# Two of the four weight sums of each FFN block by accumulating DMAs instead of VectorE adds

## The chip, the cores and the metric

The kernel runs on one core of one Trainium2 chip. The metric is the device time of one execution in microseconds, from three executions. A profile of one execution shows every instruction of the core's engines: PE is TensorE's matmuls and PEld its weight loads, DVE is VectorE, ACT is ScalarE, POOL is GpSimd, and SP is SyncE, which here only issues DMAs.

## What is computed

Two encoder layers over 256 tokens of width 2048: a recurrent and dilated-attention mixer, then a differential-attention mixer, each followed by a dense SwiGLU FFN with 5632 hidden columns. The change touches the FFN alone:

```python
D_MODEL = 2048
SEQ = 256
D_FF = -(-8 * D_MODEL // (3 * 256)) * 256

def swiglu(h, w_gate, w_up, w_down):
    return (jax.nn.silu(h @ w_gate) * (h @ w_up)) @ w_down
```

## The kernel before, in words

Everything is float32. A weight tile is 512 x 512 (1 MiB, 128 partitions of 2048 elements). Each tile is loaded from HBM by SP into a buffer `raw`, split by ACT into a rounded high part `w_hi` (four buffers, `hi`) and by DVE into the remainder `w_lo` (three buffers, `lo`), and TensorE makes three passes: high times high, high times low, low times high. A pass over 128 tokens is 4 matmuls of 128x512.

The FFN has 11 blocks of 512 hidden columns per layer. The first gate and up block of a layer is made ahead of the loop; a *body* (`block(body)` on each engine, 10 per layer, 20 in all) multiplies block j by its down weights (units `d0` to `d3`) and makes gate and up of block j+1. The contraction over 2048 is four row groups of 512, named by a digit: `g0` to `g3` are the gate tiles, `u0` to `u3` the up tiles. Groups 2 and 3 are plain *dense units* (both token halves t = 0 and 1, 24 matmuls). Groups 0 and 1 go by a seven-product scheme on the 2x2 blocks (token half by row group; row group by gate or up): products `P1` to `P7` of 12 matmuls each. `P1`, `P2`, `P3` use the plain tiles g0, g1, u1. The other four use sums and differences of the four tiles, made by `form` on DVE, each one add or subtract of 128x2048: P5 and P6 in g0's buffer, P7 (from u0 and u1) in u0's buffer, P4 (the sum of all four, with g1 as the last) in g0's buffer again.

The matching sums of the activations are made once per layer (`left_sums` on GpSimd). The partial products are combined per body: `copy_first` and `copy_fifth` on ACT, `second`, `third` and `corner` on DVE, `spreads` on GpSimd.

The order of the work in a body is written out by hand: the table `ENTRIES` sets TensorE's order and numbers the units, the calls `high(...)` and `low(...)` set ACT's and DVE's, and `LOADS` sets the order of SP's loads. All engines work their queues strictly in order. Five tile buffers (`raw0` to `raw2`, `gx`, `queries`) are handed out by `place_loads`: each load takes the buffer whose last reader comes first, and waits for that reader (`released`). The accumulator banks are `acc00`, `acc01`, `acc10`, `acc11` (second digit: token half) and `sc`, `pv`. P7 goes into `acc01`. `third` reads it there, and only then may the token half 1 of the up column write that bank; `open_bank` holds this wait:

```python
if name == first_of(column, t):
    n = body.gate if column == "g" else body.up
    pe.wait_ge(acc_free[n % 2][t], n // 2)
    if t:
        pe.wait_ge(sum_done, body.sum["S2" if column == "g" else "S3"])
```

Lines of the profile that matter: L931 is ACT's `hi`, L1527 DVE's `lo`, L1540, L1542, L1545 and L1547 are the DVE adds that form the tiles of P5, P6, P7 and P4, L1826 is `second`, L1832 `third`, L1840 `corner`, L1263 a matmul of a dense unit, L1276 one of the products P1 to P7, L796 SP's load, L2030 and L2032 GpSimd's `spreads`.

Of the kernel before, what the change touches and what calls it, by code (L numbers as in the profile page):

```python
# [94 lines left out]
        self.b = self.block_e = self.block_m = None  # L95

ENTRIES = ("P1", "P5", "P3", "P6", "g2", "P2", "P7", "P4", "u3", "g3", "u2", "d0", "d1", "d2", "d3")
LOADS = ("u1", "u0", "g0", "g2", "g1", "u3", "g3", "u2", "d0", "d1", "d3", "d2")
EARLY = ("g0", "u0")  # L100
FORMS = ("P5", "P6", "P7", "P4")
SUMS = ("S2", "S3")
PLAIN = {"P1": "g0", "P2": "g1", "P3": "u1"}

# [176 lines left out]
def hi(u):  # L281
    return Task("hi", u=u)
# [244 lines left out]
def place_loads(plan):  # L527

    count, free = [0] * BLOCK_RAW, [()] * BLOCK_RAW

    def take(key, buffers, released):
        buf = min(buffers, key=lambda i: max((when for _, _, when in free[i]), default=-1))
        count[buf] += 1
        plan.place[key] = Place(buf, count[buf], [wait[:2] for wait in free[buf]])
        free[buf] = released

    def released(body, name):
        lo_of = {entry: ("lo", u + 1, u) for entry, u in body.u.items()}
        form_of = {entry: ("form", n, body.u[entry] - 1) for entry, n in body.form.items()}
        return {"g0": (lo_of["P4"],), "u0": (lo_of["P7"],), "u1": (lo_of["P3"], form_of["P7"]),  # L540
                "g1": (lo_of["P2"], form_of["P4"])}.get(name) or (lo_of[name],)

    for part in plan.parts:
        for task in part.tasks or ():
            if task.kind == "early_load":
                take((task.src.index, task.what), range(RAW, BLOCK_RAW), released(task.src, task.what))
            elif task.kind == "tile_unit" or task.kind == "half" and task.t == 0 and task.passes[0] == 0:
                take(task.slot.u, range(RAW), (("lo", task.slot.u + 1, task.slot.u),))
        for body in part.bodies or ():
            for name in loads_of(body):  # L550
                take((body.index, name), range(BLOCK_RAW), released(body, name))
            for name in FORMS:
                plan.formed[body.u[name]] = body.form[name]
            for name in ENTRIES:
                weight = {"P4": "g0", "P5": "g0", "P6": "g0", "P7": "u0"}.get(name) or PLAIN.get(name, name)
                plan.place[body.u[name]] = plan.place[body.index, weight]

def trunk(nc, x, norm_mix_pre, norm_mix_post, norm_ffn_pre, norm_ffn_post,
# [9 lines left out]
    with ExitStack() as ctx:  # L569
# [144 lines left out]
        rg_sum = sem("rg_sum")  # L714
        rg_hi = sem("rg_hi")
        form_done = sem("form_done")
        left_part = sem("left_part")
        left_sum = sem("left_sum")
        left_hi_done = sem("left_hi_done")
# [65 lines left out]
        def _(sp):  # L785
# [5 lines left out]
            def load(key, src):  # L791

                place = plan.place[key]
                for what, value in place.free:
                    sp.wait_ge(lo_done if what == "lo" else form_done, value)
                sp.dma_start(raw[place.buf][:, :, :], src.rearrange("(k p) n -> p k n", p=P)).then_inc(landed[place.buf], 16)  # L796

            def input_chunk(c):
# [102 lines left out]
        def _(act):  # L901
# [18 lines left out]
                for kt in range(c * KT, (c + 1) * KT):  # L920
                    tile_hi(kt)

            def hi(u, formed=0):
                place = plan.place[u]
                if formed:
                    act.wait_ge(form_done, formed)
                else:
                    act.wait_ge(landed[place.buf], 16 * place.count)
                if u >= HI:
                    act.wait_ge(unit_done, u - HI + 1)  # L930
                act.activation(w_hi[u % HI][:, :, :], raw[place.buf][:, :, :], ACT.Copy).then_inc(hi_done, 1)  # L931
# [217 lines left out]
            def block(body):  # L1149

                def high(name):
                    hi(body.u[name], body.form.get(name, 0))

                def high_next(name):
                    u = body.base + len(ENTRIES) + ENTRIES.index(name)
# [30 lines left out]
                block_hi(body)  # L1186
                high("P2")
                high("P7")
                high("P4")
                high("u3")  # L1190
                high("g3")
                high("u2")
                high("d0")
# [304 lines left out]
        def _(dve):  # L1498
# [31 lines left out]
            def form(body, name):  # L1530

                def weight(which):
                    place = plan.place[body.index, which]
                    dve.wait_ge(landed[place.buf], 16 * place.count)
                    return raw[place.buf][:, :, :]

                g0 = raw[plan.place[body.index, "g0"].buf][:, :, :]
                if name == "P5":
                    up = weight("u0")
                    dve.tensor_tensor(g0, up, g0, ALU.subtract).then_inc(form_done, 1)  # L1540
                elif name == "P6":
                    dve.tensor_tensor(g0, weight("u1"), g0, ALU.subtract).then_inc(form_done, 1)  # L1542
                elif name == "P7":
                    up = weight("u0")
                    dve.tensor_tensor(up, weight("u1"), up, ALU.subtract).then_inc(form_done, 1)  # L1545
                else:
                    dve.tensor_tensor(g0, weight("g1"), g0, ALU.subtract).then_inc(form_done, 1)  # L1547

            def operand_lo(e, m, hi_ap, lo_ap):
                dve.wait_ge(t_hi, m + 1)  # L1550
# [257 lines left out]
            def block(body):  # L1808
# [11 lines left out]
                def second():  # L1820

                    dve.wait_ge(unit_done, body.u["P6"] + 1)
                    dve.wait_ge(copied[0], body.index + 1)
                    if not body.first:
                        dve.wait_ge(spread, 2 * body.index)
                    dve.tensor_tensor(spare[1], acc[1][1][:, :], spare[0], ALU.add).then_inc(sum_done, 1)  # L1826

                def third():

# [4 lines left out]
                def corner(column, t, other, out):  # L1834
# [2 lines left out]
                    wait_last(dve, body, column, t)  # L1837
                    if (column, t) != ("g", 0):
                        dve.wait_ge(spread, 2 * body.index + (1 if (column, t) == ("u", 0) else 2))
                    dve.tensor_tensor(out, acc[n % 2][t][:, :], other, ALU.add).then_inc(acc_free[n % 2][t], 1)  # L1840

                def gated(t):

# [11 lines left out]
                low("P3")  # L1855
                low("P6")
                low("g2")
                form(body, "P7")
                second()
                low("P2")  # L1860
                form(body, "P4")
                low("P7")
                low("P4")
                low("u3")
                third()
                low("g3")
                low("u2")
# [30 lines left out]
        def _(pool):  # L1898
# [100 lines left out]
            def left_sums(b, layer):  # L1999
# [12 lines left out]
                whole(spare[1], 0, 1)  # L2012
                whole(spare[0], 1, 1)
                pool.wait_ge(left_part, done + 2)
                pool.tensor_tensor(spare[0], spare[0], spare[1], ALU.add).then_inc(left_sum, 1)
                whole(spare[2], 0, 0)
                pool.wait_ge(left_part, done + 3)
                pool.tensor_tensor(spare[3], spare[2], spare[1], ALU.subtract).then_inc(left_sum, 1)
                pool.wait_ge(left_sum, done + 2)
                pool.tensor_tensor(spare[2], spare[0], spare[2], ALU.subtract).then_inc(left_sum, 1)  # L2020
                whole(spare[1], 1, 0)
                pool.wait_ge(left_part, done + 4)
                pool.wait_ge(left_sum, done + 3)
                pool.tensor_tensor(spare[1], spare[1], spare[2], ALU.subtract).then_inc(left_sum, 1)

            def spreads(body):

# [6 lines left out]
            for section in plan.parts:  # L2034
                for task in section.tasks or ():
                    task_of(task)
                for body in section.bodies or ():
                    spreads(body)

# [39 lines left out]
```

## Time and profile before

| | |
|---|---|
| timed executions | 2217.74, 2217.95, 2219.11 us (median 2217.95) |
| span of the profiled execution, first to last instruction | 2217.0 us (the profile gives no other time of its own for it) |
| TensorE busy, granted clock | 99% of the span, 0.998 of full speed |
| DVE, ACT, GpSimd busy | 76%, 53%, 14% |
| one body in the steady state | 63.65 us (P1 at 743.80 to P1 at 807.46) |
| loads | 395 MiB, SP's queue, 54.8% of the 16 DMA engines |

The span stands for the time: it lies 0.95 us under the median. A matmul record overlaps the next one, so TensorE's busy share does not show how dense it is; the distance from start to start does. Idle time of an engine that nothing waits for costs nothing.

### The profile page before, as it was taken

The page shows a single profiled execution, that of the slowest core. Times are in us where ns is not written, and L with a number is a line of the kernel's source. Part 1 is how long each engine was busy: PE and PEld are TensorE (multiplying, and loading weights), DVE is VectorE, ACT ScalarE, POOL GpSimd, SP SyncE. Part 2 cuts the span into 40 slices and gives each one's busy share as a digit, 9 for nine tenths or more (in the row PEclk, how much of TensorE's full clock was granted, in tenths as well). Part 3 has the DMA queues.
Part 4 walks back from the last instruction along what each step waited for, and adds up shares of the span by engine and source line. Part 5 has one row for each costly group of instructions (what it writes and reads, how often), then busy time and mean ns, then how long its engine had stood idle before and what let it go on. Part 6 is the DMA issues. An engine that isn't in the chain of part 4 may idle for free.

```text
span 2217.0 us, 26301 instructions
## 1 busy us (share of the span) xinstructions
PE 2199.2 (99%) x10011; PEld 1810.1 (82%) x10011; DVE 1692.9 (76%) x1686; ACT 1173.1 (53%) x1330; POOL 304.2 (14%) x247
## 2 busy tenths in 40 slices
PE   8999999999999999999999999999999999999998
PEld 7888888888888888888887787788888888888886
DVE  5587467988888888888755655778888898888886
ACT  6677544654454454444655555546555454544543
POOL 0851000300000000000021001004000000000001
PEclk9999999999999999999999999999999999999999
DMA  9555446456656555564564445455656545566552
GB/s 309 186 169 169 166 133 209 152 191 228 227 190 208 191 172 186 192 228 175 167 209 152 152 152 166 169 190 179 228 190 218 198 169 175 189 228 227 190 190 95
DMA packets 213883, 416.52 MB, mean 188 GB/s; under 512 B 12328, under 2 KB 14976, under 8 KB 213248
## 3 DMA queue, kind: packets, MB, share of 16 engines
q1 hardware_dynamic: 213040, 414.29, 54.8%
q8 instruction: 81, 1.33, 0.2%
q10 hardware_dynamic: 720, 0.56, 0.1%
q14 instruction: 42, 0.34, 0.0%
HBM read 412.73 MB, written 2.10 MB: 187 GB/s over the span
## 4 chain that ended last, share of the span: by engine, by line
PE 97%; DVE 1%; DMA 1%; issue 0%; ACT 0%; SPq 0%; POOLq 0%; POOL 0%; DVEq 0%; ACTq 0%
PE acc L1263 73%; PE acc L1276 12%; PE tp L1292 2%; PE sc L1276 2%; PE pv L1276 2%; PE sc L1374 1%; DMA raw<-in_ev_w_in 1%; PE pv L1403 1%; PE sc L1370 1%; PE pv L1398 1%; PE sc L1353 0%; PE pv L1353 0%; DVE w_lo L1527 0%; SPq L789 0%; PE pv L1292 0%
## 5 line engine op out<-in xcount | busy, mean ns | idle before, releaser
L1527 DVE TENSOR_TENSOR w_lo<-raw,w_hi 128x2048 fp32r<-128x2048 f32 x301 | 689.5, 2304 | 57.7 <-PE acc L1263 40.8
L931 ACT ACTIVATE w_hi<-raw 128x2048 fp32r<-128x2048 f32 x301 | 572.9, 1911 | 152.4 <-PE acc L1263 105.9
L1263 PE MATMUL acc<-w_hi,h_hi 128*128 128x512 f32 x1576 | 432.6, 396 | 3.8 <-ACT h_hi L903 3.8
L1263 PE MATMUL acc<-w_lo,h_hi 128*128 128x512 f32 x1576 | 423.1, 390 | 0.0
L1263 PE MATMUL acc<-w_hi,h_lo 128*128 128x512 f32 x1576 | 422.1, 390 | 0.0
L1263 PEld LDWEIGHTS acc<-w_lo,h_hi 128*128 128x128 f32 x1576 | 296.0, 188 | 62.7
L1263 PEld LDWEIGHTS acc<-w_hi,h_lo 128*128 128x128 f32 x1576 | 295.6, 188 | 61.9
L1263 PEld LDWEIGHTS acc<-w_hi,h_hi 128*128 128x128 f32 x1576 | 291.2, 188 | 63.4 <-issue 6.9
L931 ACT ACTIVATE w_hi<-gx 128x2048 fp32r<-128x2048 f32 x70 | 134.4, 1920 | 221.0 <-DVE gx L1540 83.8
L931 ACT ACTIVATE w_hi<-queries 128x2048 fp32r<-128x2048 f32 x70 | 134.4, 1920 | 220.4 <-DVE queries L1540 83.9
L1263 PE MATMUL acc<-w_hi,y_hi 128*128 128x512 f32 x832 | 224.6, 392 | 0.7 <-ACT y_hi L1135 0.7
L1263 PE MATMUL acc<-w_lo,y_hi 128*128 128x512 f32 x832 | 222.7, 389 | 0.0
L1263 PE MATMUL acc<-w_hi,y_lo 128*128 128x512 f32 x832 | 222.5, 389 | 0.0
L2030 POOL TENSOR_TENSOR probT<-probT,rgx 128x512 f32<-128x512 f32 x20 | 40.8, 2039 | 1137.1 <-ACT rgx L1170 1137.1
L1607 DVE TENSOR_TENSOR yacc<-acc,yacc 128x512 f32<-128x512 f32 x208 | 138.9, 686 | 75.8 <-PE acc L1263 75.8
L1263 PEld LDWEIGHTS acc<-w_lo,y_hi 128*128 128x128 f32 x832 | 156.1, 188 | 32.7
L1263 PEld LDWEIGHTS acc<-w_hi,y_lo 128*128 128x128 f32 x832 | 156.2, 188 | 32.6
L1263 PEld LDWEIGHTS acc<-w_hi,y_hi 128*128 128x128 f32 x832 | 155.0, 188 | 33.2 <-issue 1.9
L1527 DVE TENSOR_TENSOR w_lo<-gx,w_hi 128x2048 fp32r<-128x2048 f32 x70 | 160.0, 2286 | 7.9 <-ACT w_hi L931 7.9
L1527 DVE TENSOR_TENSOR w_lo<-queries,w_hi 128x2048 fp32r<-128x2048 f32 x70 | 160.0, 2286 | 7.9 <-ACT w_hi L931 7.9
L1840 DVE TENSOR_TENSOR prob<-acc,prob 128x512 f32<-128x512 f32 x20 | 13.8, 692 | 100.3 <-PE acc L1263 100.3
L1276 PE MATMUL acc<-w_hi,lefts 128*128 128x512 f32 x320 | 88.1, 397 | 0.0
(240 smaller groups left out, 2321.8 us busy)
## 6 DMA issues: line engine op xcount, KB each, us to landing
raw<-in_ffn_w_gate SPq DMA_DIRECT2D x68, 1024.0 KB, 5.8
raw<-in_ffn_w_up SPq DMA_DIRECT2D x68, 1024.0 KB, 5.2
raw<-in_ffn_w_down SPq DMA_DIRECT2D x48, 1024.0 KB, 7.7
raw<-in_od_w_in SPq DMA_DIRECT2D x48, 1024.0 KB, 5.1
raw<-in_ev_w_in SPq DMA_DIRECT2D x37, 1024.0 KB, 5.4
queries<-in_ffn_w_down SPq DMA_DIRECT2D x20, 1024.0 KB, 6.9
gx<-in_ffn_w_down SPq DMA_DIRECT2D x20, 1024.0 KB, 7.0
raw<-in_ev_w_out SPq DMA_DIRECT2D x16, 1024.0 KB, 5.1
```

The source lines that it names most:

```text
L931: act.activation(w_hi[u % HI][:, :, :], raw[place.buf][:, :, :], ACT.Copy).then_inc(hi_done, 1)
L1263: mm = pe.matmul(acc[n % 2][t][:, :], operand(lhs, a, k, t), w[:, k, :], start=first and k == 0 and j == 0, stop=last and k == KT - 1 and ...
L1276: mm = pe.matmul(bank, a[:, k, :], w[:, k, :], start=start and k == 0 and j == 0, stop=stop and k == KT - 1 and j == 2)
L1292: ins = pe.transpose(dst, src, ident[:, :])
L1370: mm = pe.matmul(sc[:, t, :], q[:, kt, t * P:(t + 1) * P], k[:, kt, task.i % 2, :], start=True, stop=True)
L1374: mm = pe.matmul(sc[:, :, :].rearrange("p m t -> p (m t)"), q[:, kt, t * P:(t + 1) * P], k[:, kt, :, :].rearrange("p m t -> p (m t)"), sta ...
L1398: mm = pe.matmul(pv[:, 0, t * HD:(t + 1) * HD], probT[:, j, t * P:(t + 1) * P], v[:, j, task.i * HD:(task.i + 1) * HD], start=j == 0, stop ...
L1403: mm = pe.matmul(pv[:, 0, 0:CV], flat_pt[:, j * P:(j + 1) * P], v[:, j, hd * CV:(hd + 1) * CV], start=j == 0, stop=j == 1)
L1527: dve.tensor_tensor(w_lo[u % LO][:, :, :], raw[plan.place[u].buf][:, :, :], w_hi[u % HI][:, :, :].bitcast(F32), ALU.subtract).then_inc(lo_ ...
L1607: dve.tensor_tensor(y, a, y, ALU.add).then_inc(acc_free[n % 2][t], 1)
L1840: dve.tensor_tensor(out, acc[n % 2][t][:, :], other, ALU.add).then_inc(acc_free[n % 2][t], 1)
L2030: pool.tensor_tensor(spare[1], spare[1], spare[3], ALU.add).then_inc(spread, 1)
```

## The change

The signs of u0 and g1 (and of the activations and outputs that go with them) are turned, so that all four weight tiles are sums: P5 is u0 + g0, P6 adds u1, P7 is u0 + u1, P4 is P6's tile + g1. P7's and P4's tiles are no longer formed by DVE. GpSimd issues one DMA for each, from one buffer to another in SBUF, that adds its source to its destination: `up_sum` (u1 onto u0, after P5's tile is formed) and `whole_sum` (g1 onto g0's buffer, after the low part of P6's tile has been taken). ACT's `hi` of P7 and P4 waits for the DMA's semaphore, and so do the loads that reuse u1's and g1's buffers. In the orders of TensorE, ACT and DVE, P4 and u3 change places, so that P4 comes one dense unit later. Signs in `left_sums`, `second` and `corner` follow.

```diff
-ENTRIES = ("P1", "P5", "P3", "P6", "g2", "P2", "P7", "P4", "u3", "g3", "u2", "d0", "d1", "d2", "d3")
+ENTRIES = ("P1", "P5", "P3", "P6", "g2", "P2", "P7", "u3", "P4", "g3", "u2", "d0", "d1", "d2", "d3")
-FORMS = ("P5", "P6", "P7", "P4")
+FORMS = ("P5", "P6")
+TRANSFERS = ("P7", "P4")
...
+        form_of.update({entry: (entry, 16 * (body.index + 1), body.u[entry] - 1) for entry in TRANSFERS})
...
-                sp.wait_ge(lo_done if what == "lo" else form_done, value)
+                sp.wait_ge(transferred[what] if what in TRANSFERS else lo_done if what == "lo" else form_done, value)
...
-            def hi(u, formed=0):
+            def hi(u, formed=0, moved=None):
                 place = plan.place[u]
-                if formed:
+                if moved:
+                    act.wait_ge(*moved)
+                elif formed:
...
                if name == "P5":
                     up = weight("u0")
-                    dve.tensor_tensor(g0, up, g0, ALU.subtract).then_inc(form_done, 1)
-                elif name == "P6":
-                    dve.tensor_tensor(g0, weight("u1"), g0, ALU.subtract).then_inc(form_done, 1)
-                elif name == "P7":
-                    up = weight("u0")
-                    dve.tensor_tensor(up, weight("u1"), up, ALU.subtract).then_inc(form_done, 1)
+                    dve.tensor_tensor(g0, up, g0, ALU.add).then_inc(form_done, 1)
                 else:
-                    dve.tensor_tensor(g0, weight("g1"), g0, ALU.subtract).then_inc(form_done, 1)
+                    dve.tensor_tensor(g0, weight("u1"), g0, ALU.add).then_inc(form_done, 1)
...
                 low("g2")
-                form(body, "P7")
                 second()
                 low("P2")
-                form(body, "P4")
                 low("P7")
+                low("u3")
                 low("P4")
-                low("u3")
                 third()
...
+            def up_sum(body):
+
+                place = plan.place[body.index, "u1"]
+                pool.wait_ge(landed[place.buf], 16 * place.count)
+                place = plan.place[body.index, "u0"]
+                pool.wait_ge(landed[place.buf], 16 * place.count)
+                pool.wait_ge(form_done, body.form["P5"])
+                pool.dma_start(raw[place.buf][:, :, :], raw[plan.place[body.index, "u1"].buf][:, :, :], accum_op=ALU.add).then_inc(transferred["P7"], 16)
+
+            def whole_sum(body):
+
+                place = plan.place[body.index, "g1"]
+                pool.wait_ge(landed[place.buf], 16 * place.count)
+                pool.wait_ge(lo_done, body.u["P6"] + 1)
+                pool.dma_start(raw[plan.place[body.index, "g0"].buf][:, :, :], raw[place.buf][:, :, :], accum_op=ALU.add).then_inc(transferred["P4"], 16)
...
                 for body in section.bodies or ():
+                    up_sum(body)
+                    whole_sum(body)
                     spreads(body)
```

TensorE's order in the second body, from P7 to the start of g3, before. `acc01` is the bank that `third` reads, and `sum_done` is the semaphore that `third` raises.

```order
L1276 MATMUL acc01<-w_hi2,lefts 128x512 [waits hi_done,left_lo_done,acc_free01]
...
L1276 MATMUL acc11<-w_hi3,h_hi 128x512 [waits hi_done]
...
L1276 MATMUL acc11<-w_lo2,h_hi 128x512 [waits lo_done]
...
L1263 MATMUL acc00<-w_hi0,h_hi 128x512 [waits hi_done]
...
L1263 MATMUL acc01<-w_hi0,h_hi 128x512 [waits hi_done,acc_free01,sum_done]
```

And in the change:

```order
L1282 MATMUL acc01<-w_hi2,lefts 128x512 [waits hi_done,left_lo_done,acc_free01]
...
L1269 MATMUL acc00<-w_hi3,h_hi 128x512 [waits hi_done]
...
L1269 MATMUL acc01<-w_hi3,h_hi 128x512 [waits hi_done,acc_free01,sum_done]
...
L1282 MATMUL acc11<-w_hi0,h_hi 128x512 [waits hi_done]
...
L1282 MATMUL acc11<-w_lo0,h_hi 128x512 [waits lo_done]
```

The unit that writes acc01 again (u3) now follows P7 directly; before, the 12 matmuls of P4 (acc11) lay between.

DVE's order at the same place, from the tile of P6 to `third`, before:

```order
L1542 TENSOR_TENSOR gx<-raw0,gx 128x2048 [waits landed0]
L1527 TENSOR_TENSOR w_lo0<-raw0,w_hi1 128x2048 [waits unit_done,hi_done]
L1527 TENSOR_TENSOR w_lo1<-gx,w_hi2 128x2048 [waits unit_done,hi_done]
L1527 TENSOR_TENSOR w_lo2<-raw1,w_hi3 128x2048 [waits unit_done,hi_done]
L1545 TENSOR_TENSOR queries<-raw0,queries 128x2048 [waits landed0,landed4]
L1826 TENSOR_TENSOR probT<-acc11,prob 128x512 [waits spread,copied0,unit_done]
L1527 TENSOR_TENSOR w_lo0<-raw2,w_hi0 128x2048 [waits unit_done,hi_done]
L1547 TENSOR_TENSOR gx<-raw2,gx 128x2048 [waits landed2]
L1527 TENSOR_TENSOR w_lo1<-queries,w_hi1 128x2048 [waits unit_done,hi_done]
L1527 TENSOR_TENSOR w_lo2<-gx,w_hi2 128x2048 [waits unit_done,hi_done]
L1527 TENSOR_TENSOR w_lo0<-raw1,w_hi3 128x2048 [waits unit_done,hi_done]
L1832 TENSOR_TENSOR rgx<-acc01,probT 128x512 [waits sum_done,unit_done]
```

And in the change:

```order
L1548 TENSOR_TENSOR raw2<-queries,raw2 128x2048 [waits landed4]
L1533 TENSOR_TENSOR w_lo0<-queries,w_hi1 128x2048 [waits unit_done,hi_done]
L1533 TENSOR_TENSOR w_lo1<-raw2,w_hi2 128x2048 [waits unit_done,hi_done]
L1533 TENSOR_TENSOR w_lo2<-raw1,w_hi3 128x2048 [waits unit_done,hi_done]
L1827 TENSOR_TENSOR probT<-prob,acc11 128x512 [waits spread,copied0,unit_done]
L1533 TENSOR_TENSOR w_lo0<-gx,w_hi0 128x2048 [waits unit_done,hi_done]
L1533 TENSOR_TENSOR w_lo1<-raw0,w_hi1 128x2048 [waits unit_done,hi_done]
L1533 TENSOR_TENSOR w_lo2<-raw1,w_hi2 128x2048 [waits unit_done,hi_done]
L1533 TENSOR_TENSOR w_lo0<-raw2,w_hi3 128x2048 [waits unit_done,hi_done]
L1833 TENSOR_TENSOR rgx<-acc01,probT 128x512 [waits sum_done,unit_done]
```

The two adds are gone, and the last `lo` ahead of `third` is now P4's (from raw2, the buffer that the DMA adds into), where before it was u3's.

GpSimd's order in the change, two bodies, where before only the two TENSOR_TENSOR rows stood:

```order
L2032 DMA raw0<-queries 128x2048 [waits form_done,landed0,landed4]
L2039 DMA raw2<-gx 128x2048 [waits lo_done,landed3]
L2045 TENSOR_TENSOR probT<-probT,rgx 128x512 [waits sum_done,copied1]
L2047 TENSOR_TENSOR rgx<-rgx 128x512 [waits spread]
L2032 DMA raw1<-raw0 128x2048 [waits form_done,landed1,landed0]
L2039 DMA gx<-raw2 128x2048 [waits lo_done,landed2]
```

Nothing on GpSimd waits for a DMA's end. On SP, the load of g3 waits for the DMA of P7, and one of the loads of d0, d1 for that of P4, where before g3 and u2 waited for DVE's adds.

## Rows read from the trace of the kernel before

**Rows 1.** The page, busy time of each engine over the span.

```profile
PE 2199.2 (99%) x10011; PEld 1810.1 (82%) x10011; DVE 1692.9 (76%) x1686; ACT 1173.1 (53%) x1330; POOL 304.2 (14%) x247
```

**Rows 2.** Waits of TensorE, the whole span: us in total, times, longest us.

```profile
PE acc L1263 <- ACT h_hi L903: 3.8, 1, 3.8
...
PE acc L1276 <- DVE w_lo L1527: 1.4, 2, 0.7
PE acc L1263 <- ACT y_hi L1135: 0.7, 2, 0.3
```

**Rows 3.** Windows: us, then PE, PEld, DVE, ACT, POOL busy, PEclk, DMA share, GB/s.

```profile
743.80:807.46 63.66, 63.66 (x288) 52.65 (x286) 53.38 (x38) 31.27 (x21) 5.35 (x2) 1.00 0.57 198
807.46:871.11 63.65, 63.65 (x288) 52.64 (x285) 53.38 (x38) 31.27 (x21) 5.35 (x2) 1.00 0.57 198
...
752.70:766.00 13.30, 13.30 (x60) 10.96 (x59) 13.13 (x8) 7.87 (x5) 0.00 (x0) 1.00 0.82 278
```

**Rows 4.** Timeline of TensorE in one body: start us, us, instruction.

```profile
743.80 1.17 PE L1276 MATMUL sc<-w_hi,h_hi 128*128 128x512 f32 x4
...
763.04 1.10 PE L1276 MATMUL acc<-w_hi,lefts 128*128 128x512 f32 x4
...
765.85 1.08 PE L1276 MATMUL acc<-w_hi,h_hi 128*128 128x512 f32 x4
...
768.58 1.07 PE L1263 MATMUL acc<-w_hi,h_hi 128*128 128x512 f32 x4
769.49 1.07 PE L1263 MATMUL acc<-w_lo,h_hi 128*128 128x512 f32 x4
```

**Rows 5.** Timeline of DVE, same body.

```profile
735.29 2.28 DVE L1540 TENSOR_TENSOR gx<-queries,gx 128x2048 f32<-128x2048 f32 x1
...
748.22 2.29 DVE L1527 TENSOR_TENSOR w_lo<-gx,w_hi 128x2048 fp32r<-128x2048 f32 x1
750.42 2.28 DVE L1527 TENSOR_TENSOR w_lo<-raw,w_hi 128x2048 fp32r<-128x2048 f32 x1
752.62 2.28 DVE L1545 TENSOR_TENSOR queries<-raw,queries 128x2048 f32<-128x2048 f32 x1
...
757.89 2.28 DVE L1547 TENSOR_TENSOR gx<-raw,gx 128x2048 f32<-128x2048 f32 x1
...
766.70 0.68 DVE L1832 TENSOR_TENSOR rgx<-acc,probT 128x512 f32<-128x512 f32 x1
```

**Rows 6.** Timeline of ACT, same body: high parts of P7 and of P4.

```profile
754.94 1.93 ACT L931 ACTIVATE w_hi<-queries 128x2048 fp32r<-128x2048 f32 x1 [1.83 <-DVE queries L1545]
760.21 1.93 ACT L931 ACTIVATE w_hi<-gx 128x2048 fp32r<-128x2048 f32 x1 [3.34 <-DVE gx L1547]
```

**Rows 7.** Timeline of SP's queue, same body: loads of u3 and g3.

```profile
752.73 0.37 SPq L796 DMA_DIRECT2D raw<-in_ffn_w_up  x1
754.98 0.37 SPq L796 DMA_DIRECT2D raw<-in_ffn_w_gate  x1
```

**Rows 8.** The page: the load queue, and the loads' time to landing.

```profile
q1 hardware_dynamic: 213040, 414.29, 54.8%
...
raw<-in_ffn_w_up SPq DMA_DIRECT2D x68, 1024.0 KB, 5.2
```

**Rows 9.** Timeline of GpSimd, same body.

```profile
778.95 2.04 POOL L2030 TENSOR_TENSOR probT<-probT,rgx 128x512 f32<-128x512 f32 x1 [58.22 <-ACT rgx L1170]
781.07 3.31 POOL L2032 TENSOR_TENSOR rgx<-rgx 128x512 f32<-128x512 f32 x1
```

**Rows 10.** Timeline of the first body of layer 0.

```profile
431.66 2.28 DVE L1527 TENSOR_TENSOR w_lo<-gx,w_hi 128x2048 fp32r<-128x2048 f32 x1
431.80 1.20 PE L1276 MATMUL acc<-w_lo,lefts 128*128 128x512 f32 x4 [0.71 <-DVE w_lo L1527]
...
436.17 0.37 SPq L796 DMA_DIRECT2D raw<-in_ffn_w_up  x1
...
444.71 1.10 PE L1276 MATMUL acc<-w_hi,lefts 128*128 128x512 f32 x4
```

More of the change, by code:

```diff
@@ L716, in trunk @@
         form_done = sem("form_done")
+        transferred = {name: sem(f"transferred_{name}") for name in TRANSFERS}
         left_part = sem("left_part")
@@ L1151, in high @@
                 def high(name):
-                    hi(body.u[name], body.form.get(name, 0))
+                    moved = (transferred[name], 16 * (body.index + 1)) if name in TRANSFERS else None
+                    hi(body.u[name], body.form.get(name, 0), moved)
                 def high_next(name):
@@ L1188, in block @@
                 high("P7")
+                high("u3")
                 high("P4")
-                high("u3")
                 high("g3")
@@ L1825, in second @@
                         dve.wait_ge(spread, 2 * body.index)
-                    dve.tensor_tensor(spare[1], acc[1][1][:, :], spare[0], ALU.add).then_inc(sum_done, 1)
+                    dve.tensor_tensor(spare[1], spare[0], acc[1][1][:, :], ALU.subtract).then_inc(sum_done, 1)
                 def third():
@@ L1839, in corner @@
                         dve.wait_ge(spread, 2 * body.index + (1 if (column, t) == ("u", 0) else 2))
-                    dve.tensor_tensor(out, acc[n % 2][t][:, :], other, ALU.add).then_inc(acc_free[n % 2][t], 1)
+                    dve.tensor_tensor(out, acc[n % 2][t][:, :], other, ALU.add if column == "g" else ALU.subtract).then_inc(acc_free[n % 2][t], 1)
                 def gated(t):
@@ L2014, in left_sums @@
                 pool.wait_ge(left_part, done + 2)
-                pool.tensor_tensor(spare[0], spare[0], spare[1], ALU.add).then_inc(left_sum, 1)
+                pool.tensor_tensor(spare[0], spare[0], spare[1], ALU.subtract).then_inc(left_sum, 1)
                 whole(spare[2], 0, 0)
@@ L2019, in left_sums @@
                 pool.wait_ge(left_sum, done + 2)
-                pool.tensor_tensor(spare[2], spare[0], spare[2], ALU.subtract).then_inc(left_sum, 1)
+                pool.tensor_tensor(spare[2], spare[0], spare[2], ALU.add).then_inc(left_sum, 1)
                 whole(spare[1], 1, 0)
```

## The prediction

> **What bounds the kernel now.** I read the page first: TensorE is busy 99% of the span, DVE 76%, GpSimd 14% [rows 1]. Busy time does not say how dense TensorE is, so I took TensorE's waits next. Over the whole span it waits for another engine some 6 us in all, and for DVE 1.4 us, in two places [rows 2]. Those two are the first body of each layer, where P3's low pass waits for its `lo` [rows 10], ahead of everything that the change takes off DVE. The windows then give the steady body: 63.65 us, the same twice, TensorE busy throughout, at the full granted clock (2.4 GHz) [rows 3]. A pass of 4 matmuls takes 0.91 us from start to start, a token half of a dense unit three passes, 2.72 us, and P4 2.73 us [rows 4]. Nothing in a body waits for DVE, though DVE is busy 53.4 of 63.7 us. So TensorE's own rate sets the time, and the change leaves its matmuls as they are. What can move the time is only a wait that the change makes.
>
> **Removed: two adds per body on DVE.** 2 x 2.28 us [rows 5], 91 us over 20 bodies. They lie beside matmuls, and TensorE's waits show nobody who gets them back: worth nothing. DVE now stands idle ahead of `second`, which needs P6's product.
>
> **Added: the transfer for P7.** It may start when P5's tile is formed, at 735.29 + 2.28 = 737.6 [rows 5]. ACT takes P7's tile at 754.94 [rows 6], so 17 us cover it. Without that cover its whole time would fall on P7. The load of g3 waits for it too, and now goes out right behind u3's load (752.73) instead of at 754.98 [rows 7]. That matters below.
>
> **Added and moved: the transfer for P4.** Here cover is short, because of what queues behind the wait. ACT waits for the transfer; DVE's `lo` of P4 waits for ACT; `third` stands behind that `lo` on DVE; and `third` must have read acc01 before u3's second token half may write it. u3 now starts where P4 did, at 765.85, and its second half 2.72 us later, at 768.57. Counted back from there: `third` 0.68 and hand-over 0.06; `lo` 2.20 to the next start; hi 1.93 and hand-overs 0.07 [rows 5, 6]. The transfer must have landed by 763.6. It is issued when `lo` of P6 ends, 748.22 + 2.29 = 750.5, so by 750.6. **It has 13.0 us.** By the same chain `lo` of u3 precedes that of P4 on DVE, another 2.20 us, so u3's tile must have landed by 761.4. Its load is issued at 752.73: **it has 8.7 us**, and takes 5.2 today [rows 8].
>
> **What a transfer costs.** The trace of before has no accumulating DMA and no DMA out of SBUF. The nearest row is the 1 MiB load. The queue's 54.8% of the span for 414.29 MB is 3.07 us of the 16 engines for one load, and 5.2 - 3.07 = 2.1 us is fixed [rows 8]. Low end: the price of a load, 5.2 us. An accumulate reads two tiles and writes one, so I take twice the engine time, 6.14 us, and the 2.1 us, with 0.4 us for GpSimd's issue as SP's rows have it [rows 7]: 8.6 us with the engines to itself. High end: GpSimd's own add, 3.31 us for a quarter of a tile, 13.3 us for a whole one [rows 9]. I take the middle value, since the load is the nearer row.
>
> The Trainium skill (DMA: Bandwidth & Descriptors, "Anatomy of one DMA") gives a GpSimd-issued DMA 2.0 us plus bytes by 436 GB/s. Two reads would come to 6.8 us by an estimate from it, and the transfer would then be hidden; its 4.4 us for a plain MiB is less than the 5.2 of the row.
>
> The engines are not idle there: from 752.7 to 766.0 the DMA share is already 0.82 [rows 3]. Two bounds for the sharing, since no row shows two busy queues. With **equal shares**, the transfer has 1.7 us alone before u3's load comes, and its other 4.4 us run at half speed: 0.4 + 2.1 + 1.7 + 8.9 = 13.1 us against 13.0, late by 0.1; u3's load takes 2.1 + 6.14 = 8.3 of its 8.7. With the **transfer ahead**, it is in time, and u3's load finds the engines taken for 0.4 + 6.14 - 2.1 = 4.4 us: 9.6 against 8.7, late by 0.9. I take the middle, 0.5 us per body: 18 steady bodies, 9.0 us.
>
> **The first bodies.** There `lo` of P6 ends at 431.66 + 2.28 = 433.9 and P7 starts at 444.71 [rows 10], 10.8 us later, where the steady body has 12.5 (750.5 to 763.04 [rows 4, 5]). Cover is 1.8 us shorter for both, with hand-overs: 1.9 late with equal shares, 2.7 with the transfer ahead. Middle 2.3, twice: 4.6 us.
>
> **At nothing, and why.** ACT's wait holds g3's high part behind it, which TensorE needs after u3 and P4, 8.2 us later. SP's load that waits for P4's transfer is one of d0 and d1, used over 15 us on. GpSimd issues and goes on; its `spreads` end at 784.4 [rows 9], ahead of the next P5 tile. Sums instead of differences cost DVE the same row. The load queue's other tiles come up to 6 us later and have that much.
>
> **The sum.** 2217.0 + 9.0 + 4.6 = 2230.6 us of span. The span lay 0.95 us under the median of the runs, so I forecast **2231.5 us**, 0.6% slower. About 0.2% (4.4 us) is what a measurement of this kernel can tell from no change.
>
> **Rivals.**
>
> *Not slower: the transfer is hidden* (0.36). If the engine time of an accumulate is 5 us or less, equal shares land it by 0.4 + 2.1 + 5 + 3.3 = 10.8 us, over 2 us early, and the first bodies are at most about 0.5 to 2 us late. For it: the read of SBUF may be quicker than that of HBM, and my own case misses the deadline by tenths. Against it: two reads, and a busy DMA window. Time 2217 to 2221. It decides at some 5.5 us of engine time.
>
> *Much slower: the DMA's adder is slow* (0.16). From 9.2 us of engine time (three loads) the transfer takes 0.4 + 2.1 + 1.7 + 2 x 7.5, 19.2 us with equal shares, 6 us late; with the transfer ahead 11.7 us, in time, but u3's load is 4 us late. 20 bodies: +80 to +125, so 2298 to 2343, and above 2370 at GpSimd's own rate. Only the far row [rows 9] speaks for it.
>
> *Late descriptors* (0.08). GpSimd's two adds of equal size take 2.04 and 3.31 us [rows 9], so something holds it at times, and DVE is busy 13.13 of 13.30 us in the window [rows 3]. If GpSimd must wait one DVE instruction (2.28 us) before it can start the DMA, all 20 bodies are 2.3 us later than my sum: +46, 2277. Against it: DVE has a pause of over 2 us ahead of `second` now.
>
> The Trainium skill (SBUF — State Buffer, "Who interferes with whom") has GpSimd blocked by DVE for such instructions only where GpSimd reads SBUF, and takes descriptor writing to be spared by adds with two SBUF inputs; so by the page this rival would not come about, and no row here shows a descriptor being written.
>
> *Faster* (0.02). Freed DVE time could at most give back TensorE's waits for it, 1.4 us [rows 2]: 2216.5, inside the noise. More than 4.4 us would need an effect that no row shows.
>
> **How the numbers follow.** The forecast's case, late by a few tenths to some two us per body (2222 to 2260), has 0.38. Slower by over 0.2% is 0.38 + 0.16 + 0.08, less 0.02 for the edge at 2222: 0.60. Within 0.2%: 0.36 and that 0.02: 0.38. Faster: 0.02. The range runs from the hidden case, 2216.5, to 2290, which takes in the late descriptors and leaves out nearly all of the slow adder and the 0.02 below. Slower cases hold the most; the likeliest one's own range is 2222 to 2260.
>
> **What would show it.** TensorE's waits should have a new row, a dense matmul waiting for `third` on DVE, about 18 of equal length near 0.5 us and two longer, and the body should read some 64.1 us. ACT's wait ahead of P4's high part should end on the DMA, and that DMA should take 12 to 14 us from issue to landing, the one for P7 8 to 9. A body of 63.65 us with P4's transfer under 13 us shows the hidden case. Both transfers over 13 us show the slow adder, P7's being nearly alone. A wait ahead of u3's high part on its load, with the transfer in time, shows the transfer-ahead sharing. I am wrong in the chain itself if TensorE waits elsewhere, such as on g3 or the down tiles. A body under 63.5 us would mean that something sets the rate that I take as fixed.

## The result, and the profile after

The change takes **2241.76 us** (median of 4 runs, 2241.51 to 2242.12), the kernel before 2217.93 beside it: 1.0107 times as long, 95% interval 1.0095 to 1.0119. The profiled execution took 2242.12 us, with a span of 2240.3, 23.3 us above that of before.

The page of the change, its busy times, queues and issues:

```profile
PE 2207.8 (99%) x10011; PEld 1808.7 (81%) x10011; DVE 1607.8 (72%) x1646; ACT 1168.8 (52%) x1330; POOL 339.0 (15%) x287
...
q1 hardware_dynamic: 213040, 414.29, 53.6%
q0 software_dynamic: 5760, 41.95, 10.1%
...
raw<-in_ffn_w_up SPq DMA_DIRECT2D x80, 1024.0 KB, 7.6
...
raw<-raw POOLq DMA_DIRECT2D x16, 1024.0 KB, 7.0
...
queries<-gx POOLq DMA_DIRECT2D x8, 1024.0 KB, 8.2
```

DVE lost 85 us of work against [rows 1], the 40 adds that the diff takes away. Queue q0 is new: 40 transfers, whose 10.1% of the span makes 5.66 us of the 16 engines for one, in the mean of P7's and P4's. P7's land in 7.0 us (the raw<-raw row), P4's in 8.2. The loads of `ffn_w_up`, u3's among them, went in the median from 5.2 us to landing [rows 8] to 7.6; u3's alone take 9.1 to 10.8.

TensorE's waits in the change, against [rows 2]:

```profile
PE acc L1269 <- issue: 9.5, 19, 0.7
PE acc L1269 <- DVE w_lo L1533: 5.9, 7, 1.1
PE acc L1269 <- ACT h_hi L906: 2.4, 1, 2.4
...
PE acc L1282 <- DVE w_lo L1533: 1.4, 2, 0.7
PE acc L1269 <- ACT w_hi L936: 1.0, 1, 1.0
```

Nineteen short waits for "issue" (time in which the profile names nothing that TensorE waited for), seven for a low part, and one for a high part are new. The 1.4 us of P3's low pass stay. Windows from one P7 to the next, in the change (columns as in [rows 3]); the first row is the first body of layer 0, the last that of layer 1:

```profile
443.49:511.43 67.94, 65.85 (x285) 53.62 (x284) 49.14 (x35) 32.13 (x22) 7.09 (x4) 0.97 0.71 228
511.43:575.71 64.28, 63.91 (x286) 52.57 (x284) 49.14 (x35) 31.03 (x22) 7.08 (x4) 1.00 0.73 229
639.99:705.93 65.94, 64.23 (x286) 52.48 (x284) 49.14 (x35) 32.10 (x22) 7.09 (x4) 1.00 0.72 225
...
1579.62:1645.73 66.11, 64.25 (x286) 52.41 (x285) 49.14 (x35) 31.02 (x21) 7.11 (x4) 1.00 0.74 233
```

Read so for all 20 bodies, against the same stretches of before (63.65 us, the first bodies 63.72): 13 steady bodies are longer by 0.54 to 0.80 us (0.66 in the mean), 5 by 1.2 to 2.3 (9.4 us together), the first bodies by 4.2 and 2.4. That is 8.6 + 9.4 + 6.6 = 24.6 us, and all that lies ahead of the first P7 came out 1.2 us shorter (443.49 against 444.71). So the 23.3 us are all in the FFN bodies. This is how one of the 13 loses its time, from the timeline of layer 1's third body, sorted by engine:

```profile
1699.54 0.85 POOL L2039 DMA_DIRECT2D gx<-raw  x1 [12.23 <-DVE w_lo L1533]
...
1701.03 0.37 SPq L799 DMA_DIRECT2D queries<-in_ffn_w_up  x1
1701.49 1.29 SPq L799 DMA_DIRECT2D raw<-in_ffn_w_gate  x1
...
1710.33 1.92 ACT L936 ACTIVATE w_hi<-queries 128x2048 fp32r<-128x2048 f32 x1 [7.12 <-DMA queries<-in_ffn_w_up]
1712.15 1.90 ACT L936 ACTIVATE w_hi<-gx 128x2048 fp32r<-128x2048 f32 x1
...
1712.28 2.29 DVE L1533 TENSOR_TENSOR w_lo<-queries,w_hi 128x2048 fp32r<-128x2048 f32 x1 [3.82 <-ACT w_hi L936]
1714.49 2.28 DVE L1533 TENSOR_TENSOR w_lo<-gx,w_hi 128x2048 fp32r<-128x2048 f32 x1
1716.69 0.68 DVE L1833 TENSOR_TENSOR rgx<-acc,probT 128x512 f32<-128x512 f32 x1
...
1715.96 1.07 PE L1269 MATMUL acc<-w_hi,h_lo 128*128 128x512 f32 x4
1717.48 1.17 PE L1269 MATMUL acc<-w_hi,h_hi 128*128 128x512 f32 x4 [0.45 <-issue]
```

GpSimd issues P4's transfer at 1699.54; it lands at 1707.8 (8.2 us). u3's load is issued at 1701.03 and lands 9.3 us later, at 1710.3, and ACT has waited 7.12 us for it, not for the transfer. From there it is the chain of the prediction: u3's high part, its low part, P4's low part, `third`, and TensorE starts u3's second token half 1717.48, when `third` (which ends at 1717.37) has read acc01.

Why the load took 9.3 us is in the windows of the same body:

```profile
1699.54:1700.90 1.36, 1.36 (x7) 1.09 (x6) 1.36 (x1) 1.36 (x2) 0.85 (x1) 1.00 0.00 0
1701.00:1706.50 5.50, 5.50 (x26) 4.56 (x25) 3.13 (x3) 2.21 (x2) 0.00 (x0) 1.00 1.07 185
1707.50:1710.00 2.50, 2.50 (x13) 2.07 (x12) 0.96 (x1) 0.00 (x0) 0.00 (x0) 1.00 1.04 402
```

### The profile page after: what moved, and what is told of

It is laid out like the page before. It is cut to its first block, busy times and chain, and to the rows that moved or that the text cites. A ratio compares the mean times of both kernels' runs of the same rounds, so it can differ in the third digit from the quotient of the medians.

```text
span 2240.3 us, 26321 instructions
## 1 busy us (share of the span) xinstructions
PE 2207.8 (99%) x10011; PEld 1808.7 (81%) x10011; DVE 1607.8 (72%) x1646; ACT 1168.8 (52%) x1330; POOL 339.0 (15%) x287
## 3 DMA queue, kind: packets, MB, share of 16 engines
q0 software_dynamic: 5760, 41.95, 10.1%
## 4 chain that ended last, share of the span: by engine, by line
PE 90%; DMA 4%; DVE 3%; ACT 1%; issue 1%; SPq 1%; ACTq 0%; POOLq 0%; POOL 0%; DVEq 0%
PE acc L1269 71%; PE acc L1282 9%; DMA raw<-in_ffn_w_up 3%; PE tp L1298 2%; PE sc L1282 2%; DVE w_lo L1533 2%; PE pv L1282 2%; PE sc L1380 1%; ACT w_hi L936 1%; PE pv L1409 1%; PE sc L1376 1%; PE pv L1404 1%; DMA raw<-in_ev_w_in 1%; DVE gx L1548 0%; PE sc L1359 0%
## 5 line engine op out<-in xcount | busy, mean ns | idle before, releaser
L1533 DVE TENSOR_TENSOR w_lo<-raw,w_hi 128x2048 fp32r<-128x2048 f32 x303 | 696.9, 2304 | 155.3 <-ACT w_hi L936 96.7
L1533 DVE TENSOR_TENSOR w_lo<-queries,w_hi 128x2048 fp32r<-128x2048 f32 x68 | 155.4, 2285 | 16.5 <-ACT w_hi L936 13.9
L1043 ACT ACTIVATE probT<-tp 128x256 f32<-128x256 f32 (+1 forms) x48 | 21.9, 456 | 110.5 <-PE pv L1409 64.3
```

What stands on the lines that cost most here:

```text
L1043: act.activation(flat_pt[:, 0:cols], flat_tp[:, 0:cols], ACT.Copy).then_inc(tp_free[task.e % 2], 1)
L1533: dve.tensor_tensor(w_lo[u % LO][:, :, :], raw[plan.place[u].buf][:, :, :], w_hi[u % HI][:, :, :].bitcast(F32), ALU.subtract).then_inc(lo_ ...
```

## The experiments

Theory A: P4's transfer holds the DMA engines, u3's load waits behind it, and the chain over `third` passes that on. B: not the transfer, but g3's load crowds u3's, since P7's transfer releases it 0.5 us behind u3's instead of 2.2. C: the order, with `third` behind P4's low part, costs by itself. Ratios are to the kernel before, run on the same chip.

### Parts of the change alone

```diff
-FORMS = ("P5", "P6")
-TRANSFERS = ("P7", "P4")
+FORMS = ("P5", "P6", "P7", "P4")
+TRANSFERS = ()
...
                 low("g2")
+                form(body, "P7")
                 second()
                 low("P2")
+                form(body, "P4")
                 low("P7")
...
-                    up_sum(body)
-                    whole_sum(body)
```

Both sums by DVE. 

> Undoes both transfers: DVE forms P7 and P4 again, at the places they had before, as sums; the turned signs and P4 behind u3 stay. A (P4's transfer takes the engines from u3's load): 2217.9, within 0.1% of before, u3's load back at 5.2 us. B (g3's load, released earlier by P7's transfer, crowds u3's load): 2217.9 too, since g3's load waits for DVE again. C (the order costs: third behind the low part of P4, a unit later): some 0.6 us per body stay, 2229 or more.

Measured 1.0006 (0.9997 to 1.0015), `ffn_w_up` loads 5.2 us. With P4's half of this edit alone (P7 by transfer):

> Only P7's sum by transfer; P4's by DVE as before, but P4 behind u3. A: no transfer near u3's load, so it lands in under 8.7 us and the time is 2218 to 2220. B: g3's load still goes out 0.5 us behind u3's, so u3's load stays slow (over 8.7 us) and most of the 24 us stay, 2235 or more.

Measured 0.9998 (0.9989 to 1.0007). With P7's half alone (P4 by transfer):

> Only P4's sum by transfer; P7's by DVE as before, which sends g3's load out some 2 us later than in the change. A: u3's load still finds the engines taken until 7.3 us behind the issue of the transfer, every body is late as in the change, 2235 to 2242. B: u3's load lands in time, 2218 to 2222. In between, near 2230, if the transfer makes the common 0.6 us per body and g3's load the bodies with 2.3 us.

Measured 1.0104 (1.0089 to 1.0120). The queue of the transfers in the run with P7's alone, then in the one with P4's alone:

```profile
q0 software_dynamic: 2880, 20.97, 4.7%
```

```profile
q0 software_dynamic: 2880, 20.97, 5.5%
```

Over spans of 2215.5 and 2241.4 us, that is 5.2 us of the 16 engines for one of P7's transfers and 6.2 us for one of P4's, the same kind of sum on the same number of bytes, but with u3's load issued just behind it.

The three settle it between A, B and C. C is out by the first. P7's transfer is free, and P4's alone costs all. B falls with the second, in whose timeline g3's load still goes out 0.46 us behind u3's, and u3's tile is there 5.3 us after its issue:

```profile
1683.03 0.37 SPq L799 DMA_DIRECT2D queries<-in_ffn_w_up  x1
1683.49 0.45 SPq L799 DMA_DIRECT2D raw<-in_ffn_w_gate  x1
...
1688.36 1.92 ACT L936 ACTIVATE w_hi<-queries 128x2048 fp32r<-128x2048 f32 x1 [3.15 <-DMA queries<-in_ffn_w_up]
```

### The chain over third

```diff
                 low("u3")
+                third()
                 low("P4")
-                third()
```

> The change with two of DVE's instructions swapped: third ahead of the low part of P4. A: u3's load and its low part are as late as in the change, but third no longer waits for them through P4's low part; the bodies with 0.6 us lose it, those whose low part of u3 comes too late for TensorE keep 0.6 to 1.3 us: 2224 to 2229. If the stall is elsewhere than in third: unchanged, 2241 to 2242.

Measured 1.0037 (1.0023 to 1.0052), 2227.15 us, within the expectation. TensorE's waits of this run have no "issue" row any more:

```profile
PE acc L1269 <- DVE w_lo L1533: 5.2, 6, 1.1
...
PE acc L1269 <- ACT w_hi L936: 0.9, 1, 0.9
```

So the 9.5 us that the change's profile puts down to "issue" were waits for `third`. What is left is u3's low part, late in the first bodies and in those where u3's load takes over 10 us (10.3 to 10.7 in this run).

### Holding the load, holding the transfer

g3's load held until u3's has landed:

```diff
                 for what, value in place.free:
                     sp.wait_ge(...)
+                if isinstance(key, tuple) and key[1] == "g3":
+                    early = plan.place[key[0], "u3"]
+                    sp.wait_ge(landed[early.buf], 16 * early.count)
                 sp.dma_start(raw[place.buf][:, :, :], ...)
```

> The change with one more wait on SP: g3's load goes out once u3's load has landed. A: u3's load still starts behind the transfer, but then has the engines alone and lands some 0.4 us sooner in the common bodies (10.8 to 10.4 us behind the transfer's issue) and 1.9 us sooner in those where it took over 10 us (12.3 to 10.4): 2222 to 2228, and no body with 2.3 us. If the 10 us loads have another cause than g3's load: 2234 or more. B alone (transfer harmless): u3's load under 6 us, 2218.

Measured 1.0094 (1.0079 to 1.0109), 2239.40 us: a miss for the 2222 to 2228 of A, and inside its alternative. The common bodies gained 0.1 to 0.2 us, and the long ones stayed, so the 10 us loads are not g3's doing either. Windows of one of them in this run, where u3's load is the only DMA left:

```profile
636.00:637.50 1.50, 1.50 (x8) 1.24 (x7) 0.56 (x1) 0.00 (x0) 0.00 (x0) 1.00 1.09 415
637.50:638.00 0.50, 0.50 (x4) 0.42 (x3) 0.00 (x0) 0.00 (x0) 0.00 (x0) 1.00 0.42 156
638.25:639.25 1.00, 1.00 (x6) 0.80 (x6) 0.00 (x0) 0.00 (x0) 0.00 (x0) 1.00 0.07 12
```

Nearly all of the load is done by 638; the rest has a share of 0.07, about 1/16, so I read it as one engine that ran late and brings the last pieces alone. Loads of over 10 us come in the same five bodies (the first, fourth and seventh of layer 0, the second and fifth of layer 1) in the change, in this run and in the swap above. In the change alone, the ninth body of layer 1 has a fairly long load too, of 9.8 us. Their cause stays open.

P4's transfer held until u3's load has landed:

```diff
                 pool.wait_ge(lo_done, body.u["P6"] + 1)
+                late = plan.place[body.index, "u3"]
+                pool.wait_ge(landed[late.buf], 16 * late.count)
                 pool.dma_start(...)
```

> The change with P4's transfer held until u3's load has landed. A: u3's load is back at 5 to 8 us and in time, but the transfer lands 8.2 us behind it, 15.5 to 18.5 us behind the low part of P6 where 13.0 is the budget: 2.5 to 5.5 us late in each of 20 bodies, 2268 to 2330, TensorE waiting for third, and ACT for the transfer. If the chain over third does not bind: under 2230.

Measured 1.0509 (1.0493 to 1.0524), 2331.83 us, 1.8 us beyond the far end of the expectation. Now ACT waits for the transfer and TensorE behind it (rows of one body; the wait is again `third`):

```profile
1763.37 1.92 ACT L936 ACTIVATE w_hi<-queries 128x2048 fp32r<-128x2048 f32 x1 [3.06 <-DMA queries<-in_ffn_w_up]
1772.29 1.92 ACT L936 ACTIVATE w_hi<-gx 128x2048 fp32r<-128x2048 f32 x1 [7.00 <-DMA gx<-raw]
...
1777.23 2.05 PE L1269 MATMUL acc<-w_hi,h_hi 128*128 128x512 f32 x4 [3.09 <-issue]
```

The wait itself is 3.1 us; the four matmuls behind it take 2.05 us instead of 1.08, with the granted clock at its lower level (1.2 GHz). The twenty waits sum to 71.9 us of the 113 lost. The mean granted clock of the run is 0.979, of the one of before 0.998, and 0.019 of 2331 us is 44 us: about the rest, by this estimate.

The same hold, with `third` ahead of P4's low part:

> P4's transfer held until u3's load has landed, and third ahead of P4's low part on DVE. Then only TensorE's own start of P4, 2.7 us behind that of u3's second half, waits for the transfer, and third is off the chain: budget about 18.7 us against 15.5 to 18.5. A: 2218 to 2222, the whole cost gone with both transfers kept. If the transfer's place costs something else (the down tiles' loads behind it): 2225 or more.

Measured 1.0052 (1.0035 to 1.0068), 2230.33 us: outside the 2218 to 2222, though not for the reason that its alternative gives. All 18 steady bodies are free of waits (63.65 us each); the rest is in the first bodies, where P7 starts sooner behind P6's low part and the held transfer comes too late for P4 itself:

```profile
PE acc L1282 <- ACT w_hi L936: 6.3, 2, 3.8
```

So I held it in the steady bodies alone (the two lines under `if not body.first:`):

> Both transfers kept, third ahead of P4's low part, and P4's transfer held until u3's load has landed, but in the 18 steady bodies alone; in the first body of each layer it starts when it can. A: the steady bodies have no wait, as with the hold in all bodies, and the first bodies are late as with third first alone, 2.3 and 1.3 us, without the 2.7 to 4.0 us and the half clock behind them that the hold made there: 2219 to 2223. It can't beat the kernel before, whose steady bodies are TensorE's own 63.65 us. If the hold moves the down tiles' loads so that first bodies suffer from it too: 2226 or more.

Measured 1.0022 (1.0013 to 1.0031), 2223.11 us, 0.1 us above the expectation. A steady body of it, to be read against [rows 3]:

```profile
511.42:575.07 63.65, 63.65 (x285) 52.64 (x284) 49.24 (x35) 31.16 (x21) 7.08 (x4) 1.00 0.73 231
```

That is before's rate again with both transfers in place. It does not beat the kernel before: in the steady bodies TensorE has no gap left to close, and the first bodies keep their waits.

### What the transfer costs, and how the engines share

P4's transfer as a plain copy (g1 over the tile), which leaves out one add per element and so changes P4's product:

```diff
-  pool.dma_start(<g0's buffer>, <g1's buffer>, accum_op=ALU.add)
+  pool.dma_start(<g0's buffer>, <g1's buffer>)
```

> P4's transfer copies g1 over the tile instead of adding it, with the same bytes written; P4's product is then that with g1 alone, and one add per element is left out. If the adding sets the 6.1 us of the engines: a copy takes about what a load does, 3.0 us, u3's load lands some 6 to 7 us behind its issue, inside its budget, and the time is 2218 to 2221. If the rows of 8 KB through GpSimd's queue are slow by themselves: the same 6.1 us, and 2241.

Measured 0.9999 (0.9989 to 1.0008), with u3's load landing in about 6.2 us, inside its 8.7. From its page:

```profile
q0 software_dynamic: 5760, 41.95, 7.5%
...
queries<-gx POOLq DMA_DIRECT2D x8, 1024.0 KB, 5.1
```

With 7.5% of 2218.3 us against 10.1% of 2240.3, a copy takes 59.9 / 20 = 3.0 us less of the engines than an accumulate and lands in 5.1 us instead of 8.2. A copy, at 6.2 less 3.0, then costs about what a load does (3.07 us), and the accumulate about one more load on top. The Trainium skill (Collectives: The Full Stack, "The bandwidth ceiling: the fold count and why AG ≠ RS ≠ AR") says of the adding step of a collective that it is slower because it reads two sources and not because of the add. The run agrees in size, without showing which of the two it is.

P4's transfer in four DMAs of 2 KB rows:

```diff
+  for k in range(KT):
+      pool.dma_start(<g0's buffer>[:, k, :], <g1's buffer>[:, k, :], accum_op=ALU.add)
```

> P4's transfer in four DMAs of 256 KB, whose rows are 2 KB instead of 8 KB. Taking turns by descriptor: with rows as long as the load's, the load gets its share of the engines, lands in 8 to 9 us instead of 9.3 to 10.8, and the transfer lands later, 11 to 13 us, near its budget: 2218 to 2232. Transfer first whatever its rows: the load starts behind the last quarter, which is issued up to 2.6 us later (0.87 us of GpSimd each): u3's load 10 to 12 us, 2245 to 2280.

Measured 1.0715 (1.0699 to 1.0731), 2377.68 us, far worse than either expectation. The sharing did come, but GpSimd could not issue the fourth (its timeline, then windows):

```profile
790.89 2.66 POOL L2040 DMA_DIRECT2D queries<-gx  x3 [11.72 <-DVE w_lo L1533]
800.93 0.86 POOL L2040 DMA_DIRECT2D queries<-gx  x1 [7.38 <-issue]
```

```profile
792.40:794.00 1.60, 1.60 (x8) 1.32 (x8) 0.15 (x1) 1.60 (x2) 1.16 (x2) 1.00 1.05 166
796.00:799.00 3.00, 3.00 (x15) 2.49 (x14) 3.00 (x2) 0.00 (x0) 0.00 (x0) 1.00 1.05 283
800.20:803.00 2.80, 2.80 (x14) 2.33 (x13) 0.53 (x1) 1.92 (x1) 0.86 (x1) 1.00 1.06 401
```

In the middle window the engines move 283 GB/s, between the transfer's 166 and the loads' 401: both are served. u3's load took 7.9 us in this body, inside its 8.7. But the fourth quarter went out 10 us behind the first, once the third had landed (at 800.67), and TensorE waited up to 7.0 us per body for `third`. To get the sharing without four DMAs, I made two of 2 KB rows (`[:, 0::2, :]` and `[:, 1::2, :]`), and for comparison two of 4 KB rows (halves):

> P4's transfer as two DMAs, of the tile's even and odd quarters, so that its rows are 2 KB and not 8 KB, without a third and fourth DMA for GpSimd to wait with. Turns by row: each engine alternates between a row of the transfer (four times shorter now) and one of the load, as they did in the quarters; the load of u3 has about half the engines from 3.7 us behind the transfer's issue, lands 7.5 to 8.3 us behind its own, inside 8.7, and the transfer lands 11 to 12 us behind its issue, inside 13.0: 2218 to 2224, the first bodies late by some 1 us each. Transfer first whatever its rows: 2241 to 2250, the second DMA's issue on top.

> P4's transfer as two DMAs, of the tile's first and second half, with rows of 4 KB. Turns by row: the load of u3 gets a smaller part of the engines than with rows of 2 KB, and lands between the two, 8.5 to 9.3 us behind its issue: 2222 to 2240. If two DMAs instead of one are what helps and not the rows: the same time as with rows of 2 KB.

Measured 1.0433 (1.0416 to 1.0450), 2315.66 us, with rows of 2 KB, and 1.0116 (1.0101 to 1.0131), 2244.95 us, with rows of 4 KB: both missed. GpSimd in the run with 2 KB rows:

```profile
779.19 1.22 POOL L2040 DMA_DIRECT2D queries<-gx  x1 [12.13 <-DVE w_lo L1533]
785.59 1.20 POOL L2040 DMA_DIRECT2D queries<-gx  x1 [5.18 <-issue]
```

The second DMA went out as the first landed, so the transfer was late, and TensorE waited for `third` (60.8 us over 20 bodies), though u3's load, at 7.3 us, was in time. And while the first ran, u3's load (issued 780.71, so with data possible from about 782.8 by the same 2.1 us) was not served at first, though the rows were as short as its own; windows of 783 to 785.2 in the same body, at whose end that DMA lands:

```profile
783.00:784.00 1.00, 1.00 (x7) 0.81 (x6) 0.94 (x2) 0.00 (x0) 0.00 (x0) 1.00 1.09 109
784.00:785.20 1.20, 1.20 (x7) 1.00 (x6) 1.20 (x1) 0.00 (x0) 0.00 (x0) 1.00 0.92 234
```

The first of them has GpSimd's slow pace alone; the load comes in only in the second, as the DMA ends. So "turns by row" is wrong: with one GpSimd DMA under way, the load is let in only as that DMA ends. With several queued, as with the quarters, it gets in from the end of the first. In the 4 KB run, two DMAs issued 0.5 us apart, the halves landed in 4.7 and 8.3 us, and u3's load still took 9.4. The Trainium skill (DMA: Bandwidth & Descriptors, "Queues, rings and completion order") has each DMA engine take turns between queues by whole packets of some 9 to 17 descriptors, and ("The descriptor swizzle") counts 9 per engine for a 1 MiB transfer from GpSimd. If so, a transfer would be one packet on each engine, and a load behind it would wait for all of it. The 185 GB/s window and the three runs here agree with that; none of them shows a packet's bounds.

## Why the prediction came out as it did

**Right: the sign and the place.** Faster was out, and "slower by over 0.2%", which had 0.60, came; 2241.76 lies in the range, 10 us above the forecast. DVE's relief (91 us forecast, 85 by the page) was worth nothing (both parts undone: 1.0006), P7's transfer was covered (7.0 us of 17). What I put at nothing cost nothing: with the hold in the steady bodies and `third` first, both transfers, g3's early load and `spreads` are still there, and the steady body is 63.65 us. The chain from u3's tile over P4's low part and `third` to u3's second half is the one in the rows. Its budget of 8.7 us fits: loads of 9.2 us made TensorE wait 0.5, and 64.1 us were expected for the body where 64.28 came.

**Near: the price of the transfer.** 6.14 us of engine time were estimated. P4's measured 6.2 beside the load, but P7's, nearly alone, 5.2. It landed in 7.0 us where I had 8.6 for a transfer alone, so the 8.2 us of P4's are near my 8.6 partly by luck: I had put no price on running beside a load. The plain copy shows that one more load's time for the accumulate was the right size. GpSimd issues P4's transfer 0.6 to 0.75 us behind the end of P6's low part, where I had it at once, and the issue takes 0.85 us, not 0.4; u3's load goes out 1.5 to 1.7 us behind the transfer's issue, not 2.1.

**Failed: the step on the sharing.** I bounded it by equal shares and by the transfer ahead, and took the middle, 0.5 us per body. There was nothing to average: in all 20 bodies the transfer went first, and u3's load took 9.1 us or more. The transfer landed in 8.2 us (median), not in 12 to 14, and the load took the whole delay. My "transfer ahead" bound, 9.6 us for the load and 0.9 late, was the mechanism, and slightly too high for the common body (9.2 us, 0.66 us lost). So ACT waits ahead of u3's high part, the alternative sign I named, and not ahead of P4's. That bound alone would have given 18 x 0.9 + 2 x 2.7 = 21.6 us, 2239.5. I had no row to choose by; the rule of the Trainium skill cited above, on packets, points to the transfer ahead, and I did not use it.

**Mis-sized: steady bodies 9.0 us, measured 18.0.** The common 13 gave 8.6. The other 9.4 us came in 5 bodies whose u3 load took 9.8 to 10.8 us, for which I had no term; why it did is open. **First bodies 4.6 us, measured 6.6.** Layer 1's lost 2.4 us, near the 2.3 forecast. Layer 0's lost 4.2: u3's load took 10.4 us there, and about half of the 4.2 is the clock, which fell behind the waits. Together 11.0 us more, less the 1.2 at the start: 9.8, against the 9.7 us by which the span missed.

**A reading that was off.** I put TensorE's waits in the kernel before at some 6 us in all. The whole list sums to 8.0: one wait of 1.5 us for GpSimd and two short ones are not in [rows 2]. These three lie in no FFN body, so nothing rests on them.

**The rivals.** I had "hidden" decide at some 5.5 us of engine time. The transfer has 5.2 nearly alone and 6.2 beside the load, on either side of it, and the plain copy, at 3.0 us less, is hidden. The slow adder (9.2 us or more) did not come. Neither did the late descriptors: P4's transfer was issued at most 0.75 us behind the low part of P6, where this rival needs 2.3. "Much slower" did come in three of the variants, by a way that I had not listed: a transfer that starts late (the hold) or in parts of which the last has to wait for an earlier one.

## What to carry to other kernels

Work moved from a compute engine to a DMA is not judged by its own deadline alone: ask which load is issued just behind it, and reckon that this load gets its data only when the transfer is done (here 9.2 us instead of 5.2). Relief for an engine that TensorE does not wait for buys nothing, so such a move needs its cost hidden completely to break even. Here that took two orders: the instruction that others wait for (`third`) ahead of the one that waits for the DMA, and the transfer behind the urgent load. With both, the steady bodies were back at 63.65 us, and the first bodies still left the kernel 1.0022 times as long as before.

## What the runs showed of the hardware

- A GpSimd accumulate of 1 MiB kept the 16 engines from the load queue nearly until it landed: 185 GB/s while it ran, 402 after.
- Accumulating from SBUF to SBUF costs 3.0 us of the 16 engines more than copying the same 1 MiB. Issued just ahead of u3's load it lands in 8.2 us, the copy in the same place in 5.1; P7's accumulate, with no load issued just behind it, lands in 7.0.
- GpSimd can't issue any number of DMAs ahead. Three DMAs of 128 rows, and two of 128, went out at once; the fourth of 128 and the second of 256 waited, for 7.4 and 5.2 us, until an earlier one had landed. So 384 rows went out together and 512 did not; no run tells whether rows or something that goes with them are counted.
- A load behind an accumulate sometimes takes 10.2 to 10.8 us instead of 9.2, in the same five bodies of several kernels; in the body shown above, the last pieces came at about one engine's share. In the trace of before, u3's load took 5.1 to 5.3 us in 19 bodies, and 5.8 in one.
- A pause of TensorE can cost more than itself. In the change's first body of layer 0 it waited 0.96 and 1.13 us close together, and then the granted clock was at its lower level (1.2 GHz):

```profile
450.30:453.70 3.40, 3.40 (x9) 2.63 (x8) 3.40 (x3) 2.52 (x2) 0.00 (x0) 0.50 1.04 373
```

Nine matmuls ran there in 3.4 us, where the full clock does 15. Waits of 0.5 us once per body left the clock at 1.00, and so did pairs nearly as long as the first: 0.97 and 0.74 us in the body from 639.99, 1.13 and 0.73 in layer 1's first. No run shows where the bound lies.
